# A mixer pass on Trainium2: norms made token by token in few columns, and a new order of scores, corners and unit keys

## What is computed

```python
kk = hd(k * rw['k_k'])
kk = kk / jnp.maximum(jnp.sqrt(jnp.sum(kk * kk, axis=-1, keepdims=True)), 1e-12)   # unit keys, heads of 64
# per direction d: decays, keys = k * (1 + (a - 1) * k_a), rates a = sigmoid(a0 + al @ a_up)
S = (S * w_t - einsum('bhvk,bhk->bhv', S, kk_t)[..., None] * (kk_t * a_t)
     + v_t[..., None] * k_t)                                                       # one token
o_t = einsum('bhvk,bhk->bhv', S, r_t)
# readout: a group norm over the 64 channels of a head
mu, var = mean(o), mean(square(o - mu))
y = (o - mu) * rsqrt(var + GN_EPS) * gn_w + gn_b + bonus
out = y * (sigmoid(glo) @ g_up)
```

## Time and profile before

| | us |
|---|---|
| median of 3 runs | 3269.04 (3264.67 to 3271.74) |
| the profiled execution | 3263.43 |
| its span | 3261.8 |
| mixer passes in it | from about 743 to 1286 |
| PE / DVE / ACT busy, of the span | 3021.5 / 2191.4 / 1253.5 |

### The profile page before, as it was taken

One profiled execution on the slowest core, in us unless ns is written; L12 is line 12 of the kernel. 1 busy time (PEld: TensorE's weight loads), 2 busy tenths in 40 slices (PEclk: granted clock), 3 DMA queues, 4 the chain that ended last, 5 costly groups with the idle time before them and its releaser, 6 DMA issues.

```text
span 3261.8 us, 49969 instructions
## 1 busy us (share of the span) xinstructions
PE 3021.5 (93%) x20896; PEld 2491.8 (76%) x20896; DVE 2191.4 (67%) x2720; ACT 1253.5 (38%) x1446; POOL 216.6 (7%) x394
## 2 busy tenths in 40 slices
PE   4999999787888887999999999999889899999999
PEld 2588987446667766788888888799867788888887
DVE  2687766477777775578787787759974555555554
ACT  1322221264444443434344444334543433434342
POOL 1000000001000100012212121100000000000000
PEclk8799999899999998999999999999989999999999
DMA  9976987790000031668888887755305556555553
GB/s 332 354 273 231 324 289 243 277 343 22 12 14 13 22 67 50 225 228 284 291 291 288 278 302 274 264 167 183 104 6 178 167 192 193 187 187 194 193 181 129
DMA packets 306012, 640.58 MB, mean 196 GB/s; under 512 B 19035, under 2 KB 23937, under 8 KB 303585
## 3 DMA queue, kind: packets, MB, share of 16 engines
q1 hardware_dynamic: 269280, 529.94, 48.0%
q0 software_dynamic: 28384, 94.76, 8.9%
q10 hardware_dynamic: 8128, 12.72, 1.1%
HBM read 623.81 MB, written 13.40 MB: 195 GB/s over the span
## 4 chain that ended last, share of the span: by engine, by line
PE 82%; DVE 9%; DMA 4%; ACT 3%; issue 1%; ACTq 0%; SPq 0%; POOLq 0%; DVEq 0%
PE ps L445 46%; PE ps L463 15%; PE ps L465 7%; DMA raw<-in_ada_w_dram 3%; PE ps L2371 2%; DVE rw_mb L1349 1%; DVE rw_mt L1352 1%; PE ps L382 1%; PE ps L1807 1%; PE ps L1759 1%; PE ps L1607 1%; PE ps L1608 1%; ACT rw_tt L1074 1%; DVE rw_scl L1332 1%; PE ps L1649 1%
## 5 line engine op out<-in xcount | busy, mean ns | idle before, releaser
L422 DVE TENSOR_TENSOR split_lo<-raw,split_hi 128x2048 fp32r<-128x2048 f32 (+1 forms) x372 | 849.8, 2286 | 495.2 <-ACT split_hi L410 487.7
L410 ACT ACTIVATE split_hi<-raw 128x2048 fp32r<-128x2048 f32 x368 | 702.2, 1912 | 1175.4 <-PE ps L445 837.2
L463 PE MATMUL ps<-xa,split_hi 128*128 128x512 f32 x2048 | 720.6, 397 | 6.7 <-ACT xa L617 6.7
L465 PE MATMUL ps<-xa,split_lo 128*128 128x256 f32 x2048 | 573.6, 280 | 0.0
L463 PEld LDWEIGHTS ps<-xa,split_hi 128*128 128x128 f32 x2048 | 384.3, 188 | 100.8 <-ACT xa L617 7.7
L445 PE MATMUL ps<-split_hi,hT_hi 128*128 128x512 f32 x1024 | 399.5, 390 | 0.0
L445 PE MATMUL ps<-split_hi,hT_lo 128*128 128x512 f32 x1024 | 398.4, 389 | 0.0
L445 PE MATMUL ps<-split_lo,hT_hi 128*128 128x512 f32 x1024 | 398.4, 389 | 0.0
L465 PEld LDWEIGHTS ps<-xa,split_lo 128*128 128x128 f32 x2048 | 386.6, 189 | 0.2
L445 PEld LDWEIGHTS ps<-split_hi,hT_hi 128*128 128x128 f32 x1024 | 192.2, 188 | 41.6 <-issue 1.8
L445 PEld LDWEIGHTS ps<-split_hi,hT_lo 128*128 128x128 f32 x1024 | 192.3, 188 | 40.1
(11 more groups left out here) (385 smaller groups left out, 4489.6 us busy)
## 6 DMA issues: line engine op xcount, KB each, us to landing
raw<-in_mlp_w_dram SPq DMA_DIRECT2D x256, 1024.0 KB, 5.4
raw<-in_ada_w_dram SPq DMA_DIRECT2D x64, 1024.0 KB, 9.6
raw<-in_mix_in_w_dram SPq DMA_DIRECT2D x48, 1024.0 KB, 5.5
raw<-in_conv_pw_w_dram SPq DMA_DIRECT2D x48, 1024.0 KB, 5.4
gate<-in_ada_w_dram SPq DMA_DIRECT2D x172, 256.0 KB, 5.0
...
```

The costliest lines, as they stand in the source:

```text
L410: nc.scalar.activation(split_hi[:, c, :, 0:n], raw[:, c, :, 0:n], ACT.Copy).then_inc(hi_done, 1)
L422: nc.vector.tensor_tensor(split_lo[:, c, :, 0:n], raw[:, c, :, 0:n], split_hi[:, c, :, 0:n], ALU.subtract).then_inc(lo_done, 1)
L463: pe.matmul(ps[:, base + j, :], split_hi[:, c, kk, j * P:(j + 1) * P], both, start=(k == 0), stop=False, skip_group_check=True)
L465: mm = pe.matmul(ps[:, base + j, 0:SEQ], split_lo[:, c, kk, j * P:(j + 1) * P], xa_hi[:, k, :], start=False, stop=(k == KT - 1), skip_grou ...
```

## The change

The norms of keys and of groups are made with the operands exchanged: the squares of 128 tokens are the weights and two columns of the block matrix stream, so a norm stands once per token and head, on the token's partition, 8 columns for the keys and 4 for the groups. Maximum and reciprocal work on these; a copy spreads each over 64 columns, and PE turns them back (`key_back`, `scale_back`), so that DVE reads the scale from PSUM. Unit keys are made inside the scan's third chunk, decayed keys in its second and third, values of the next pass in its first. All scores come before the first opening and update; the mean matmul stands after the first chunk's scores; the deviation on ACT after the packing. The diagonal blocks are written by ACT and DVE together. Turn and corner product of half 1, and its two corner copies, move into the scan. The scaled queries stand ahead of the output sums.

```diff
-SCB = [7, 2, 6, 0, 1, 3, 4, 7, 2, 6, 1, 3, 4, 7, 2, 6]
+SCB = [7, 4, 6, 0, 1, 3, 2, 7, 4, 6, 1, 3, 2, 7, 4, 6]
...
 def key_norm(x):
-    act.wait_ge(W["nrm_ps"], x.n(1, 1))
-    nc.scalar.activation(rw["t12"][:, 1, :], ps[:, prep_bank(x, 4), :], ACT.Sqrt).then_inc(W["nrm"], 1)
+    act.wait_ge(W["nrm_ps"], x.n(2, 1))
+    nc.scalar.activation(rw["t12"][:, 1, 0:8], ps[:, norm_bank(x), 0:8], ACT.Sqrt).then_inc(W["nrm"], 1)
...
+def deviation_squares(x):
+    act.wait_ge(W["om"], x.n(2, 1))
+    nc.scalar.activation(rw["t12"][:, 0, 0:SEQ], rw["o"][:, :], ACT.Square).then_inc(W["sqo"], 1)
 def deviation(x):
-    act.wait_ge(W["om"], x.n(1, 1))
-    nc.scalar.activation(rw["t12"][:, 0, 0:SEQ], rw["o"][:, :], ACT.Square).then_inc(W["sqo"], 1)
-    act.wait_ge(W["epi_ps"], x.n(3, 3))
-    nc.scalar.activation(rw["t12"][:, 0, SEQ:TOK], ps[:, EPI, SEQ:TOK], ACT.Sqrt, scale=1.0 / HD, bias=epsc[:, 1:2]).then_inc(W["sqo"], 1)
+    act.wait_ge(W["epi_ps"], x.n(4, 3))
+    nc.scalar.activation(rw["t12"][:, 0, SEQ:SEQ + 4], ps[:, EPI, SEQ:SEQ + 4], ACT.Sqrt, scale=1.0 / HD, bias=epsc[:, 1:2]).then_inc(W["sqo"], 1)
...
 def own_blocks(x, b):
     act.wait_ge(W["z_lev"], x.n(NS, NS - 1 + b))
-    for e in range(2):
-        h = own_half(e)
-        ins = nc.scalar.activation(rw["tt"][h, 2 * b:2 * b + 2, :, h].rearrange("p c i s -> p i c s"),
-                                   ps[h, ZB[b], :].rearrange("p (i c s) -> p i c s", c=2, s=HB), ACT.Copy)
-    ins.then_inc(W["zz"], 1)
+    h = own_half(0)
+    nc.scalar.activation(rw["tt"][h, 2 * b:2 * b + 2, :, h].rearrange("p c i s -> p i c s"),
+                         ps[h, ZB[b], :].rearrange("p (i c s) -> p i c s", c=2, s=HB), ACT.Copy).then_inc(W["zz"], 1)
...
-    packed(x, 0)
-    packed(x, 1)
     corners(x, 0)
     corners(x, 1)
     for k in range(NT_DVE):
         level_values(x, k)
-    last_turned(x, 0)
-    last_turned(x, 1)
+        if k >= NT_DVE - 2:
+            last_turned(x, k - (NT_DVE - 2))
     own_blocks(x, 0)
     own_blocks(x, 1)
     half_product(x, 0)
     half_product(x, 1)
-    corner_out(x, 0)
...
         if c == 0:
+            corner_out(x, 0)
             if not last:
                 rates(x.next())
+            corner_out(x, 1)
...
+    packed(x, 0)
+    if not first:
+        deviation_squares(x.last())
+    packed(x, 1)
     if not first:
         deviation(x.last())
     inverse(x)
...
+def decayed_keys(x, part):
...
+    if part == 0:
+        steps.inc(V.tensor_scalar(rw["kd"][:, :, :], rw["a"][:, :, :], cur[:, C_KA:C_KA + 1], cur[:, C_OKA:C_OKA + 1], ALU.mult, ALU.add))
+        return
+    steps.wait()
     kb = rw["k"][:, :].rearrange("p (o t) -> p o t", o=1).to_broadcast([P, 2, TOK])
     steps.inc(V.tensor_tensor(rw["kd"][:, :, :], rw["kd"][:, :, :], kb, ALU.mult))
...
-def key_scale(x, h):
-
-    if h == 0:
-        dve.wait_ge(W["nrm"], x.n(1, 1))
-        steps.link(V.tensor_scalar(t12[:, 1, :], t12[:, 1, :], 1e-12, None, ALU.max))
-    o = slice(h * SEQ, (h + 1) * SEQ)
-    steps.inc(V.reciprocal(t12[:, 0, o], t12[:, 1, o]))
+def key_scale(x):
+    dve.wait_ge(W["nrm"], x.n(1, 1))
+    steps.link(V.tensor_scalar(t12[:, 1, 0:8], t12[:, 1, 0:8], 1e-12, None, ALU.max))
+    steps.link(V.reciprocal(t12[:, 1, 8:16], t12[:, 1, 0:8]))
+    V.tensor_copy(t12[:, 0, :].rearrange("p (j s) -> p j s", s=HD),
+                  t12[:, 1, 8:16].rearrange("p (j o) -> p j o", o=1).to_broadcast([P, 8, HD])).then_inc(W["k"], 1)
...
+    dve.wait_ge(W["nrm_ps"], x.n(2, 2))
     steps.link(V.scalar_tensor_tensor(out=rw["kk"][:, :], in0=rw["k"][:, :], scalar=cur[:, C_KK:C_KK + 1],
-                                      in1=t12[:, 0, :], op0=ALU.mult, op1=ALU.mult))
+                                      in1=ps[:, norm_back_bank(x), :], op0=ALU.mult, op1=ALU.mult))
...
+def own_blocks(x, b):
+    dve.wait_ge(W["z_lev"], x.n(NS, NS - 1 + b))
+    h = own_half(1)
+    V.tensor_copy(rw["tt"][h, 2 * b:2 * b + 2, :, h].rearrange("p c i s -> p i c s"),
+                  ps[h, ZB[b], :].rearrange("p (i c s) -> p i c s", c=2, s=HB)).then_inc(W["off_d"], 1)
...
-def group_scale(x, h):
+def group_scale(x):
     dve.wait_ge(W["sqo"], x.n(2, 2))
-    steps.inc(V.reciprocal(t12[:, 1, h * P:(h + 1) * P], t12[:, 0, SEQ + h * P:SEQ + (h + 1) * P]))
+    steps.link(V.reciprocal(t12[:, 0, SEQ + 4:SEQ + 8], t12[:, 0, SEQ:SEQ + 4]))
+    V.tensor_copy(t12[:, 1, 0:SEQ].rearrange("p (j s) -> p j s", s=HD),
+                  t12[:, 0, SEQ + 4:SEQ + 8].rearrange("p (j o) -> p j o", o=1).to_broadcast([P, 4, HD])).then_inc(W["om"], 1)
 def normalised(x):
     steps.wait()
-    steps.inc(V.tensor_tensor(t12[:, 0, 0:SEQ], rw["o"][:, :], t12[:, 1, 0:SEQ], ALU.mult))
+    dve.wait_ge(W["epi_ps"], x.n(4, 4))
+    steps.inc(V.tensor_tensor(t12[:, 0, 0:SEQ], rw["o"][:, :], ps[:, EPI, SEQ:TOK], ALU.mult))
...
-        if c == 0 and not first:
+        if c == 1 and not first:
             centred(x.last())
-    masked(x, 0)
     mask_scores(x, 3)
-    for k in range(1, NS):
+    for k in range(NS):
         masked(x, k)
         if not first:
             if k == 1:
-                group_scale(x.last(), 0)
-                group_scale(x.last(), 1)
-            elif k == 2:
+                group_scale(x.last())
+            elif k == 3:
                 normalised(x.last())
-            elif k == 3:
+            elif k == 4:
                 affine(x.last())
-            elif k == 4:
+            elif k == 5:
                 with_bonus(x.last())
-            elif k == 5:
+            elif k == 6:
                 gated(x.last())
         if k == 6:
...
+    own_blocks(x, 0)
+    own_blocks(x, 1)
     turned_blocks(x, 0)
+    corner_out(x, 0)
     turned_blocks(x, 1)
-    corner_out(x, 0)
-    corner_out(x, 1)
-    if not last:
-        dve.wait_ge(W["bv"], x.n(1, 1))
-        for part in range(3):
-            shift_value(x.next(), part)
...
-        if c == 2 and not last:
-            key_scale(x.next(), 0)
...
+        if c == 0:
+            corner_out(x, 1)
         if c == 0 and not last:
-            decayed_keys(x.next())
+            dve.wait_ge(W["bv"], x.n(1, 1))
+            for part in range(3):
+                shift_value(x.next(), part)
+        if c == 1 and not last:
+            key_scale(x.next())
+            decayed_keys(x.next(), 0)
         if c == 2:
             if not last:
-                key_scale(x.next(), 1)
+                decayed_keys(x.next(), 1)
+                unit_keys(x.next())
             dve.wait_ge(W["o_ps"], x.n(2, 1))
             V.tensor_copy(rw["o"][:, :], ps[:, 2, 0:SEQ]).then_inc(W["o"], 1)
             dve.wait_ge(W["o"], x.n(2, 1))
@@ -1496,12 +1523,11 @@
     inverse(x, first, last)
     scan(x, last)
     if not last:
-        unit_keys(x.next())
         scaled_keys(x.next(), 0)
         scaled_keys(x.next(), 1)
+        dve.wait_ge(W["o_ps"], x.n(2, 2))
+        scaled_queries(x.next())
     outputs(x)
-    if not last:
-        scaled_queries(x.next())
...
 def key_norm(x):
     pe.wait_ge(W["sq"], x.n(1, 1))
-    pe.wait_ge(W["lw"], x.n(2, 1))
-    pe.matmul(ps[:, prep_bank(x, 4), :], R["blk"][:, :], R["t12"][:, 0, :], start=True, stop=True).then_inc(W["nrm_ps"], 1)
+    if x.off == 0:
+        pe.wait_ge(W["lw"], x.n(2, 1))
+    else:
+        pe.wait_ge(W["off_d"], x.last().n(6, 5))
+    for t in range(4):
+        mm = pe.matmul(ps[:, norm_bank(x), 2 * t:2 * t + 2], R["t12"][:, 0, t * P:(t + 1) * P], R["blk"][:, 0:P:HD], start=True, stop=True)
+    mm.then_inc(W["nrm_ps"], 1)
...
+def key_back(x):
+    if x.off == 0:
+        pe.wait_ge(W["cum"], x.n(4, 3))
+    pe.wait_ge(W["k"], x.n(2, 2))
+    for t in range(4):
+        tr = pe.transpose(ps[:, norm_back_bank(x), t * P:(t + 1) * P], R["t12"][:, 0, t * P:(t + 1) * P], ident[:, :])
+    tr.then_inc(W["nrm_ps"], 1)
...
 def corner(x, b):
     pe.wait_ge(W["off_a"], x.n(6, 3 + b))
-    pe.wait_ge(W["off_d"], x.n(4, 1 + b))
+    pe.wait_ge(W["off_d"], x.n(6, 3 + 2 * b))
...
 def variance(x):
     pe.wait_ge(W["sqo"], x.n(2, 1))
-    pe.matmul(ps[:, EPI, SEQ:TOK], R["blk"][:, :], R["t12"][:, 0, 0:SEQ], start=True, stop=True).then_inc(W["epi_ps"], 1)
+    for t in range(2):
+        mm = pe.matmul(ps[:, EPI, SEQ + 2 * t:SEQ + 2 * t + 2], R["t12"][:, 0, t * P:(t + 1) * P], R["blk"][:, 0:P:HD], start=True, stop=True)
+    mm.then_inc(W["epi_ps"], 1)
+def scale_back(x):
+    pe.wait_ge(W["om"], x.n(2, 2))
+    for t in range(2):
+        tr = pe.transpose(ps[:, EPI, SEQ + t * P:SEQ + (t + 1) * P], R["t12"][:, 1, t * P:(t + 1) * P], ident[:, :])
+    tr.then_inc(W["epi_ps"], 1)
...
-        if c == 0 and not first:
+        if c == 1 and not first:
             mean(x.last())
         scores(x, c, first)
-        if c == 2 and not first:
-            variance(x.last())
-        if c == 2:
-            opened(x, 0)
+    opened(x, 0)
     update(x, 0)
+    if not first:
+        variance(x.last())
     corners(x, 0)
     corners(x, 1)
     opened(x, 1)
@@ -1744,13 +1796,15 @@
```

(39 more changed lines are left out.)

17 lines of the change are left out of this document (7 added, 10 removed).

## The result

| | before | after |
|---|---|---|
| median, us | 3266.20 (5 runs, 3260.71 to 3271.74) | 3298.01 (5 runs, 3288.10 to 3301.27) |
| profiled execution | 3263.43 | 3301.05 |
| its span | 3261.8 | 3299.4 |

The change makes the kernel slower: the ratio is 1.0093 [1.0073, 1.0113], 0.9% more time, where 0.35% less was forecast. The time lies outside the range of 3247 to 3270.

A forecast was written before the change was run, and what follows sets the result against it. Eight serial passes, each a ring of hand-overs between PE, DVE and ACT, were taken as the bound. Terms of -14.8 us plus 3.5 for the clock gave 3252.1, plus 5.6 for the median 3257.7; range 3247 to 3270.

The forecast's parts named there:

- the clock: TensorE falling to half rate behind an idle stretch before the first update: six of seven passes, 1.4 us each, 3.5 more.
- End of the inverse: Last update to first scan product: shared block writes and a deferred corner cut 5.66 us to 4.45, gain 1.2.
- The scan: Scan, 1.9 us longer: second corner 0.54, moved key norms 0.94, turns 0.5, less 0.1 of idle PE.
- Their low bound: Cheapest case for the two-column key norms in the scan: 0.06 us a record, 0.4 in all.
- From the scan to the scores: After the scan, DVE is the bound; moving unit keys and output additions away gains 2.5 us.
- Scores, masks, first levels: First score to sixth level half: masks end 2.5 us earlier, but a PE chain follows; gain only 0.1 us.
- 7.9 us of PE work: PE's row from first update to the turned group scale, ahead of the normalising step, for which DVE waits.
- The third: Rival: low clock on the PE chain before normalising in every pass, up to 7.9 us each; 3304 us, chance 0.09.
- the low stretch seen cost 1.26: Argument against the low-clock rival: the profiled pass with a half-clock stretch was 1.26 us longer than its neighbour.
- The first rival: Cheap new matmuls (norms 0.4, variance 0.2) and no further clock falls; 3249 us, chance 0.15.
- The second: Rival: PE's chain ahead of the normalising step is 1.6 us longer and eats the gain; 3268 us, chance 0.14.

The follow-up runs named there:

- e2: Changed kernel with the levels' first bank opening issued three times instead of once, ahead of the first update; 3280.65 us, ratio 1.0034.
- e3: Changed kernel with key norms streaming 128 columns instead of two, and the first bank opening issued three times; 3243.71 us, ratio 0.9919.
- e1: Changed kernel with the key norms streaming 128 columns instead of two, in the same place; 3264.94 us, ratio 0.9991.
- e5: Kernel before, with four unread matmuls of two streamed columns added ahead of the decays in the scan's first chunk; 3303.95 us, ratio 1.0116.
- e6: Kernel before, with four unread matmuls of 128 streamed columns added ahead of the decays in the scan's first chunk; 3273.54 us, ratio 1.0017.

## Why the prediction was wrong

The step that failed is the clock, a term that the sum put at 3.5 us. The other steps come first, in the order of the pass.

**End of the inverse: right.** 4.66 measured, 4.45 forecast, a gain of 1.0 instead of 1.2.

**The scan: right at full clock.** It grows by 1.67 us; forecast was 1.9. The norms, for which no row of before had the shape, take 0.91 us until the next matmul starts, against 0.94. Their low bound was divided wrongly: 0.67 for 16 records is 0.04 a record and not 0.06, which changes nothing, as the norms came out at 0.11. The other terms held within 0.15. The reciprocal of eight columns is 0.20, and the copy that spreads it 0.53, within its bounds of 0.42 and 0.69:

```profile
868.12 0.20 DVE L1300 RECIPROCAL rw_t<-rw_t 128x8 f32<-128x8 f32 x1
868.36 0.53 DVE L1301 COPY rw_t<-rw_t 128x512 f32<-128x512 f32 x1
```

**From the scan to the scores: right.** The last addition to the first score took 7.70 and takes 5.14, a gain of 2.56 for a forecast of 2.5.

**Scores, masks, first levels: right at full clock.** Masks end at 9.10 (8.85), normalising at 18.47 (18.2), with the wait of DVE on PE's turn where it was announced. e2 and five passes of e3 show it, since the changed kernel itself never runs these levels at full clock. The pass is 64.4 (64.3): 1.84 us shorter, for a forecast of 1.9.

**The clock: the step that failed, twice.** It was costed at 3.5 us more, and it cost about 50.

First, the size. I took a fall in six of seven passes "at 1.4 us", about the price of those before. It came in all seven, at 3.0: 21.1 us, where the four falls of before cost 4.7. What grew is above all the stretch itself, 6.8 us at the low clock instead of 3.4. Work that others wait for lay under it before, too: in the pass of the earlier trace rows the low clock lay on the last scores and put the end of the masks off by 1.27 us, the whole loss of that pass. In the passes of e1 and e3 where the stretch behind the first update is short, it costs 1.5. So the price of a short stretch was taken for every fall, while the same text had counted 7.9 us of PE work that a longer one could lie on. Why it is longer in the new order stays open.

Second, the place. I looked for falls only behind idle stretches, and this part of the scan has none. Five of seven scans fell in the middle of continuous work, for 33.8 us. e1 against the change (33 us) and e5 against e6 (30 us) show that the streams of two columns do it in this place.

The account of the spans of the two profiled executions, in us: seven pass intervals at full clock -13.5 (six at 1.84, the last at 2.5), the low clock in the levels +21.1 - 4.7, the scans +33.8, the first scan product 2.7 later, and behind the last pass's first product 2.1 sooner. The sum is 37.3, and the spans differ by 37.6. The 2.7 are lost ahead of the first pass, where two executions of other kernels differ as much (787.7 for the first scan product in the kernel before, 792.4 in e1); the forecast had 0.3 sooner there. A small part of the miss is the median of before, put 5.6 us above its profiled execution; with five runs it is 2.8.

**The rivals.** The third, low clock on the PE row in every pass, said 3304, and 3298 was measured. Its mechanism is confirmed by e2 and e3, but its size is not: it gave 7.9 us a pass, and the chain was stretched by 3.0, so by itself it would have given 3263.4 - 14.8 + 16 = 3265 on the scale of the profiled execution. e1, which has this fall alone, measured 3264.7 there. That the rival came near the time is luck: the scan's fall, which no case had, lies on top. The argument "the low stretch seen cost 1.26" against it was the mistake above. The first rival fell: the norms are not cheap, and the clock did not stay. The second fell too, as the row was as long as counted.

The rule cited from the Trainium skill, TensorE: Matmul & The Clock Gate, Part 1 (gaps between bursts put the array back to half rate), agrees with the levels: the fall follows a gap of 2.75 us in all seven passes, and one of 1.03 in none (e2) or two (e3). It does not cover the scan, where the clock fell to 0.50 in windows with PE busy 1.00. There the measurement decides.
